# Mixers, attention, a feed-forward head and the last norm of a three-layer forward pass in another order

## The reference

```python
# first block: conformer conv, forgetting attention, short conv and pooling in parallel
mix = concatenate([y_conf, y_att, y_sc, y_pool], -1) @ w_out
h = h + rms_norm(mix, g_mix_post)
ff = square(relu(rms_norm(h, g_mlp_pre) @ w_up)) @ w_down
h = h + rms_norm(ff, g_mlp_post)
gate = sigmoid(rms_norm(h, g_ple_pre) @ w_ple_gate)
h = h + rms_norm((p @ w_ple_proj) * gate, g_ple_post)
# second block: layer 0 mixes by attention (8 latent heads, 4 differential
# heads of two maps each), layer 1 by a state-space and a gated recurrence
for l in range(2):
    m = attention_mixer(rms_norm_2(x, ...)) if l == 0 else recurrent_mixer(rms_norm_2(x, ...))
    x = x + m
    x = x + (silu(hn @ w_gate) * (hn @ w_up)) @ w_down      # width 2816
return rms_norm_2(x, norm_final)
```

## Time and profile before

| | us |
|---|---|
| runs | 1001.95, 1003.36, 999.59 |
| median | 1001.95 |
| the profiled execution's own time | 1000.06 |
| its span | 998.2 |
| PE busy | 953.5 (96%) |
| DVE busy | 700.3 (70%) |
| ACT busy | 515.8 (52%) |
| POOL busy | 87.1 (9%) |

### The profile page before, as it was taken

One profiled execution on the slowest core, in us unless ns is written; L12 is line 12 of the kernel. 1 busy time (PEld: TensorE's weight loads), 2 busy tenths in 40 slices (PEclk: granted clock), 3 DMA queues, 4 the chain that ended last, 5 costly groups with the idle time before them and its releaser, 6 DMA issues.

```text
span 998.2 us, 13575 instructions
## 1 busy us (share of the span) xinstructions
PE 953.5 (96%) x5540; PEld 835.9 (84%) x5540; DVE 700.3 (70%) x921; ACT 515.8 (52%) x698; POOL 87.1 (9%) x110
## 2 busy tenths in 40 slices
PE   6997999999999899889999999999989889999997
PEld 5996797888888688778988888888988789888886
DVE  4798785666667887886666666667979676666663
ACT  4776754444436646765543434368645355434341
POOL 4353000000000100000000000000132000000000
PEclk9999999999999999989999999999999999999999
DMA  9732365665565354224665656546321356656531
GB/s 320 245 128 92 120 220 194 199 207 183 174 206 175 112 171 143 85 85 125 215 208 173 207 171 209 169 149 211 127 85 49 121 169 211 207 172 208 172 127 43
DMA packets 106190, 164.40 MB, mean 165 GB/s; under 512 B 2816, under 2 KB 82784, under 8 KB 106000
## 3 DMA queue, kind: packets, MB, share of 16 engines
q1 hardware_dynamic: 104688, 158.25, 48.9%
q0 software_dynamic: 1440, 5.28, 1.5%
HBM read 162.47 MB, written 1.05 MB: 164 GB/s over the span
## 4 chain that ended last, share of the span: by engine, by line
PE 69%; DVE 19%; ACT 6%; issue 4%; DMA 2%; POOL 1%; DVEq 0%; POOLq 0%; ACTq 0%
PE ps L379 67%; DVE wl L1739 6%; DVE SC L1841 2%; PE ps L387 2%; ACT wh L1172 2%; DMA raw<-in_w_in 1%; DVE xhl L1744 1%; DVE xf L1748 1%; ACT junk L1160 1%; DVE st L2139 1%; ACT xhl L1178 1%; POOL st L2496 1%; DVE rows L2339 1%; DVE hs L1759 0%; DVE h L1801 0%
## 5 line engine op out<-in xcount | busy, mean ns | idle before, releaser
L1739 DVE TENSOR_TENSOR wl<-raw,wh 128x2048 fp32r<-128x2048 f32 (+2 forms) x150 | 339.6, 2266 | 153.8 <-ACT wh L1172 153.6
L1172 ACT ACTIVATE wh<-raw 128x2048 fp32r<-128x2048 f32 (+2 forms) x150 | 281.9, 1884 | 156.6 <-PE ps L379 142.8
L379 PE MATMUL ps<-xhl,wh 128*128 128x512 f32 (+1 forms) x1248 | 257.9, 354 | 2.5 <-ACT wh L1237 2.5
L379 PEld LDWEIGHTS ps<-xhl,wh 128*128 128x128 f32 x1248 | 202.4, 193 | 29.9 <-issue 3.7
L379 PE MATMUL ps<-wh,xhl 128*128 128x512 f32 (+3 forms) x1000 | 195.2, 339 | 6.0 <-ACT SC L1435 1.8
L379 PEld LDWEIGHTS ps<-wh,xhl 128*128 128x128 f32 x1000 | 155.1, 190 | 25.3 <-ACT xhl L1178 2.6
L379 PEld LDWEIGHTS ps<-xhl,wl 128*128 128x128 f32 x1008 | 135.6, 191 | 7.5
L379 PE MATMUL ps<-xhl,wl 128*128 128x256 f32 x1008 | 140.6, 282 | 0.0
L379 PE MATMUL ps<-wl,xhl 128*128 128x512 f32 (+3 forms) x500 | 105.2, 336 | 0.0
L379 PE MATMUL ps<-wh,fh 128*128 128x512 f32 x304 | 91.0, 392 | 1.8 <-DVE fl L1986 1.5
L379 PE MATMUL ps<-wh,fl 128*128 128x512 f32 x304 | 90.2, 390 | 0.0
(11 more groups left out here) (266 smaller groups left out, 840.8 us busy)
## 6 DMA issues: line engine op xcount, KB each, us to landing
raw<-in_ffn_gate SPq DMA_DIRECT2D x22, 1024.0 KB, 5.3
raw<-in_ffn_up SPq DMA_DIRECT2D x22, 1024.0 KB, 5.4
raw<-in_ffn_down SPq DMA_DIRECT2D x22, 1024.0 KB, 4.9
raw<-in_w_up SPq DMA_DIRECT2D x16, 1024.0 KB, 5.6
raw<-in_w_down SPq DMA_DIRECT2D x16, 1024.0 KB, 4.9
raw<-in_s_w_in SPq DMA_DIRECT2D x14, 1024.0 KB, 5.4
raw<-in_w_in SPq DMA_DIRECT2D x9, 1024.0 KB, 7.1
raw<-in_a_w_in SPq DMA_DIRECT2D x6, 1024.0 KB, 5.1
```

The costliest lines, as they stand in the source:

```text
L379: return e.matmul(o, a, b, start=start, stop=stop, skip_group_check=True)
L1172: e.activation(high_of(i), raw_of(i), ACT.Copy).then_inc(*up("act_high", i))
L1739: e.tensor_tensor(low_of(i), raw_of(i), high_of(i).bitcast(F32), ALU.subtract).then_inc(*up("dve_lo", i))
```

## The change

The same work is done by the same kinds of instructions, with four exceptions: four PSUM copies go from ACT to DVE, two activation table loads are added by the order on ACT, one `wl` of 128x2048 is made as two of 128x1024, and the last norm's products are shared otherwise. The rest is order, and the waits that go with it. In the diff, cut to its changed lines, the function is given ahead of each piece.

On PE: `project_end` (a wait inside it), `down_block` in halves and the order in `ffn`, `logits` and `map_back` in `attention`, `score` and `level` in `recurrent`, and the end of `recurrent`.

```diff
@@ -482 +482 @@
-def project_end(n, sl, tb, half, order):
+def project_end(n, sl, tb, half, order, x_low=None):
@@ -489,0 +490,2 @@
+            if x is xl and i == order[2] and x_low:
+                e.wait_ge(*x_low)
@@ -673 +675 @@
-    def down_block(j, tb):
+    def down_block(j, tb, halves=(0, 1)):
@@ -675 +677 @@
-        tok(down[j], [(ps[ACC[s_next][tb][c]][:, :], HALF[c]) for c in range(2)], tb, 0, j == 0, False, x)
+        tok(down[j], [(ps[ACC[s_next][tb][c]][:, :], HALF[c]) for c in halves], tb, 0, j == 0, False, x)
@@ -728,2 +730,2 @@
-        down_block(0, 0)
-        e.wait_ge(*at("dve_head", l, 1, 1))
+        down_block(0, 0, (0,))
+        e.wait_ge(*at("dve_head", l, 1, 0))
@@ -730,0 +733,2 @@
+        down_block(0, 0, (1,))
+        e.wait_ge(*at("dve_head", l, 1, 1))
@@ -732,2 +735,0 @@
-        e.wait_ge(*at("dve_head_low", l, 1, 4))
-        down_block(0, 1)
@@ -735,0 +738,2 @@
+        e.wait_ge(*at("dve_head_low", l, 1, 0))
+        down_block(0, 1)
@@ -830,0 +835,2 @@
+            e.wait_ge(*at("act_qk_turned", 1, 1, 0))
+        if i == 9:
@@ -897 +903 @@
-            e.wait_ge(*at("act_qk_turned", 1, 0, 0))
+            e.wait_ge(*at("act_qk_turned", 0, 0, 1))
@@ -1013 +1019 @@
-                e.wait_ge(*at("act_cb", tb))
+                e.wait_ge(*at("dve_cb", tb))
@@ -1028 +1034 @@
-            e.wait_ge(*at("act_xs", 0))
+            e.wait_ge(*at("dve_xs", 0))
@@ -1090 +1095,0 @@
-    feat(S["hq"][1], ps[0])
@@ -1100,0 +1106 @@
+    feat(S["hq"][1], ps[0])
@@ -1131 +1137 @@
-    e.wait_ge(*at("dve_mix3_low", 1, 0))
+    e.wait_ge(*at("act_part_high", 6, 1, 0))
@@ -1133 +1139 @@
-        project_end(6, sl, 0, half, order)
+        project_end(6, sl, 0, half, order, at("dve_mix3_low", 1, 0))
```

```diff
@@ -1312 +1318 @@
-    highs(10)
+    taps(22, 24)
@@ -1315 +1321,2 @@
-    taps(22, 26)
+    highs(10)
+    taps(24, 27)
@@ -1320 +1327 @@
-    taps(26, 29)
+    taps(27, TAPS)
@@ -1327 +1333,0 @@
-    taps(29, TAPS)
@@ -1341 +1346,0 @@
-    forget_probs(3)
@@ -1343,0 +1349 @@
+    forget_probs(3)
@@ -1561 +1567,2 @@
-    tick(7, do)
+        if c == 0:
+            tick(7, do)
@@ -1647 +1654 @@
-    for i in range(2):
+    def queries(i):
@@ -1664,0 +1672 @@
+    queries(0)
@@ -1666,3 +1673,0 @@
-    for tb in range(2):
-        e.wait_ge(*at("pe_xs", tb))
-        e.activation(xs[:, tb, :], ps[(7, 1)[tb]][:, :], ACT.Copy).then_inc(*up("act_xs", tb))
@@ -1670,3 +1674,0 @@
-    for g in range(2):
-        e.wait_ge(*at("pe_cb", g))
-        e.activation(cbs[:, g, :], ps[(2, 5)[g]][:, 0:384], ACT.Copy).then_inc(*up("act_cb", g))
@@ -1674,0 +1677 @@
+    queries(1)
@@ -1708,4 +1711,2 @@
-    for tb in range(2):
-        e.wait_ge(*at("dve_mix3_x", 1, tb))
-        part_high(4, 8, tb, (6, 1, tb))
-    norm_squares(6, 0)
+    e.wait_ge(*at("dve_mix3_x", 1, 0))
+    part_high(4, 8, 0, (6, 1, 0))
@@ -1712,0 +1714,4 @@
+    e.wait_ge(*at("dve_mix3_x", 1, 1))
+    part_high(4, 8, 1, (6, 1, 1))
+    norm_squares(6, 0)
+    highs(UP["f1"][0][1])
@@ -1726,2 +1731,6 @@
-norm_squares(7, 0)
-norm_squares(7, 1)
+for tb in range(2):
+    norm_squares(7, tb)
+    e.wait_ge(*at("pool_rstd", "norm", 7, tb))
+    e.wait_ge(*at("dve_final", tb, 1))
+    e.activation(hs[:, tb, HALF[1]], hs[:, tb, HALF[1]], ACT.Identity, scale=st[:, 3 * tb + 2:3 * tb + 3]).then_inc(
+        *up("act_out", tb))
```

```diff
@@ -1741,0 +1751,12 @@
+def low_half(i, half):
+
+    n = slots[i][1] * slots[i][2] // 2
+    c = slice(n * half, n * half + n)
+    assert i == low[0]
+    if half == 0:
+        e.wait_ge(*at("act_high", i))
+    d = e.tensor_tensor(low_of(i)[:, c], raw_of(i)[:, c], high_of(i)[:, c].bitcast(F32), ALU.subtract)
+    if half == 1:
+        d.then_inc(*up("dve_lo", i))
+        low[0] += 1
+
@@ -1910,3 +1931 @@
-    taps(11, 17)
-    lows(8)
-    taps(17, 20)
+    taps(11, 16)
@@ -1916,2 +1935 @@
-    lows(9)
-    taps(20, 23)
+    lows(8)
@@ -1919,0 +1938,2 @@
+    taps(16, 19)
+    lows(9)
@@ -1924 +1944 @@
-    taps(23, 25)
+    taps(19, 21)
@@ -1926,2 +1946 @@
-    lows(10)
-    taps(25, TAPS)
+    taps(21, TAPS)
@@ -1938 +1956,0 @@
-    mix_low(3)
@@ -1943,0 +1962 @@
+    mix_low(3)
@@ -1944,0 +1964 @@
+    lows(10)
@@ -1946 +1965,0 @@
-    lows(11)
@@ -1947,0 +1967 @@
+    lows(11)
@@ -2012 +2032 @@
-        lows(ups[3][0] + 3)
+        lows(ups[3][0] + 2)
@@ -2013,0 +2034 @@
+        lows(ups[3][0] + 3)
@@ -2016 +2036,0 @@
-        lows(down[0] + 3)
@@ -2018,0 +2039 @@
+        lows(down[0] + 3)
@@ -2165,0 +2187,4 @@
+            if i == 3:
+                low_half(S["aout"][3], 0)
+            if i == 5:
+                low_half(S["aout"][3], 1)
@@ -2226,2 +2250,0 @@
-        if t == 8:
-            lows(S["aout"][3])
@@ -2325,0 +2349,7 @@
+    lows(S["xbc"][2] + 4)
+    for tb in range(2):
+        e.wait_ge(*at("pe_xs", tb))
+        e.tensor_copy(xs[:, tb, :], ps[(7, 1)[tb]][:, :]).then_inc(*up("dve_xs", tb))
+    for g in range(2):
+        e.wait_ge(*at("pe_cb", g))
+        e.tensor_copy(cbs[:, g, :], ps[(2, 5)[g]][:, 0:384]).then_inc(*up("dve_cb", g))
@@ -2414,0 +2445,2 @@
+
+    def gated_columns_low(tb):
@@ -2417,0 +2450,3 @@
+    e.wait_ge(*at("dve_cb", 1))
+    e.wait_ge(*at("dve_dt_turned"))
+    decayed(0)
@@ -2421,0 +2457 @@
+    decayed(1)
@@ -2424,3 +2459,0 @@
-    e.wait_ge(*at("act_cb", 1))
-    decayed(0)
-    decayed(1)
@@ -2447 +2479,0 @@
-    lows(S["sout"][2])
@@ -2451 +2482,0 @@
-    state_columns(1)
@@ -2452,0 +2484,2 @@
+    state_columns(1)
+    gated_out(0)
@@ -2454,2 +2487,4 @@
-    for tb in range(2):
-        gated_out(tb)
+    gated_out(1)
+    gated_columns(0)
+    lows(S["sout"][2])
+    gated_columns_low(0)
@@ -2457,2 +2492,3 @@
-    for tb in range(2):
-        gated_columns(tb)
+    lows(UP["f1"][0][0])
+    gated_columns(1)
+    gated_columns_low(1)
@@ -2461 +2496,0 @@
-    lows(UP["f1"][0][0])
@@ -2463 +2497,0 @@
-    lows(UP["f1"][0][1])
@@ -2465 +2499 @@
-    lows(UP["f1"][1][0])
+    lows(UP["f1"][0][1])
@@ -2467 +2501 @@
-    lows(UP["f1"][1][1])
+    lows(UP["f1"][1][0])
@@ -2468,0 +2503 @@
+    lows(UP["f1"][1][1])
@@ -2484,0 +2520,3 @@
+    for c in (1, 0):
+        e.tensor_tensor(hs[:, tb, HALF[c]], h[:, tb, HALF[c]], rows[:, 1, HALF[c]], ALU.mult).then_inc(
+            *up("dve_final", tb, c))
@@ -2486,3 +2524,2 @@
-    for c in range(2):
-        e.scalar_tensor_tensor(hs[:, tb, HALF[c]], h[:, tb, HALF[c]], r, rows[:, 1, HALF[c]], ALU.mult,
-                               ALU.mult).then_inc(*up("dve_out", tb, c))
+    e.wait_ge(*at("dve_final", tb, 0))
+    e.tensor_scalar(hs[:, tb, HALF[0]], hs[:, tb, HALF[0]], r, None, ALU.mult).then_inc(*up("dve_out", tb))
@@ -2567 +2604 @@
-        e.wait_ge(*at("dve_weighed", n - 2))
+        e.wait_ge(*at("dve_weighed", max(1, n - 2)))
@@ -2601 +2638 @@
-        e.wait_ge(*at("dve_out", tb, c))
+        e.wait_ge(*(at("act_out", tb) if c else at("dve_out", tb)))
```

16 lines of the change are left out of this document (8 added, 8 removed).

## The result

The changed kernel takes 985.23 us (median of four runs, 984.29 to 985.81) against 1000.97 us of the kernel before (four runs): a ratio of 0.9839, with a 95% interval of 0.9817 to 0.9862. The forecast was 987.4, with a range of 982.0 to 996.0.

The account below looks back on a forecast made before the run. PE was taken to bound the kernel, busy 953.5 of 998.2 us, so only its idle waits could be won. Six terms summed to 14.55 us, turning the median 1001.95 into 987.4, range 982 to 996.

Parts of the forecast that it names:

- Mixer: First mixer: the conformer's mean starts at 84.8 instead of 88.47, winning 3.7 us; bounds 1.5 and 5.0.
- Head of "ff": Feed-forward head: PE's 1.53 us wait goes, a new one of 0.9 comes; net 0.65 us, from -0.7 to 1.5.
- Attention: Attention: split copies and low-part halves in DVE's gaps shorten PE's waits of 1.93 and 2.91; 3.4 us, bounds 1.5 and 4.5.
- Recurrent front: Front of recurrent layer: heads(0) 2.9 us earlier, but heads(2) limits the gain to 1.4 us; bounds -1.0 and 2.6.
- The step that named part(2) as the cause: Recurrent layer's front: DVE reaches decayed(2) at 743.6 instead of 744.8, since part(2), now waiting for weighed(1), is late.
- Recurrent tail: Tail of recurrent layer: moving wl behind needed columns removes 6.0 us of waits, adds two of 0.4; 5.2 us, bounds 3.0 and 6.0.
- Last norm: Last norm: gain products hidden under ACT's squares and POOL's power; 0.2 us won, from -0.5 to 0.5.
- which eats most of it: Last norm: POOL's power, 1.0 to 1.4 us elsewhere beside two-input DVE operations, takes most of the gain, leaving 0.2 us.
- (1): Mixer and recurrent front: DVE and POOL cost each other more than taken; gain 10.4, time 991.5; chance 0.16.
- (2): Weight stream late into "f1": the later raw load lands too late, losing the tail's 5.2; 992.7; chance 0.08.
- (3): Whole kernel: waits only move, second waits take what is freed, 3 us are left; 999; chance 0.08.
- (4): Attention or recurrent front: new gaps hold PE at 1.2 GHz; 29 us of it eats the gain, 40 gives 1007.5; chance 0.04.

Follow-up runs that it names:

- the filling products: Changed kernel plus six products of constants, overwritten by the mean, in PE's wait ahead of the conformer's mean: 983.87 us, ratio 0.9827 to the kernel before.

## Why the prediction was right, point by point

**The time.** The sum of the six terms was 14.55 us, the spans differ by 14.7, and the profiled executions' own times by 14.8 (1000.06 to 985.26). The median came out 2.2 below the forecast not through the terms but through the last step, which put the median 1.9 us above the profiled execution, as it was in three runs of the kernel before. The changed kernel's median is its profiled execution's time, within 0.03.

**Mixer, 3.7 forecast, 4.07.** Right: the turn without a wait, the mean held by the last of DVE's taps, the two small waits gone, and the hold behind the mean, put at 1.25 us and 1.09 by the filling products. PE waits there for high parts that stand behind a weight's high part on ACT; the prediction called it the third head's chain. Mis-sized: the taps. POOL ended at 81.0, not 82, and the last of DVE's ten taps ran beside an idle POOL, 0.66 us each on average (6.58/10), so the mean came at 83.9 and not 84.8. Left out: half clock behind the mean, 1.3 us in this profile. I had put the clock's fall in a rival that was to decide at 29 us of it, and not in the term itself, where a wait of 2.9 us was named by my own working. The two errors have opposite signs, so that the sum fits this well is in part luck; and the profile drew one of the two long stretches at half clock, against the median first stage the mixer gives 4.9.

**Head of "ff", 0.65, 0.79.** The new wait was put at 0.9 and is 0.70. This term was not undone by itself; the run with the mixer of before has the same 171.92.

**Attention, 3.4, 3.7.** The mix was to start at 422.7 after a wait of 2.4; shifted by the 4.84 won ahead of it, it did at 422.46 after 2.04. Both low halves were hidden. Not seen: the wait of 1.45 ahead of the turn of map 9, and that half clock shrank from 10.2 us to 3.4. PE's idle time falls by 1.5 us only; the other 2.2 are busy time, as in the upper bound, which had named the clock. The run with the attention of before has both long stretches at half clock again (414.3 to 417.8, 421.1 to 428.0). The prediction's map 7 and map 9 are the steps `tick(7)` and `tick(9)`, in which ACT takes the exponential of map 6 and DVE the maxima of map 8; no term hangs on the number.

**Recurrent front, 1.4, 1.5.** heads(0) came 3.0 us earlier, as worked out, and heads(2) 1.6, where 1.2 had been worked out. The step that named part(2) as the cause was half right: it shortens weigh(1), but undoing it costs nothing in the end. The table loads cost what their rows said.

**Recurrent tail, 5.2, 5.0.** Each of the four long waits went or shrank, the x_low wait came at 0.37, and the load that is issued later lands in time. Two small terms were wrong and offset each other in part: the two short waits of 0.9 together are not in the trace, where the stage's idle time is 5.2 in all (PE busy 55.3 of 60.5), of which the four long waits are 5.1; and the 0.4 for the wl of sout3 did not come. Without both the sum would have been 4.7.

**Last norm, +0.2, -0.3.** The only sign that was wrong. The step that failed is "which eats most of it": I had POOL's power at 1.0 to 1.4 beside DVE from other rows and still counted a gain, and did not ask what two halves that are ready at one time do to their transfers. The power took 0.93 instead of 0.55, and the last transfer landed 0.63 us behind the one before it.

**The rivals.** (1) DVE and POOL do cost each other what the rows said, but in the mixer POOL was done before it mattered. (2) No late weight: no wait for one appears in "f1". (3) The waits did not only move: PE's idle time fell from 44.8 to 33.3 us. The new or remaining ones (2.04, 1.45, 0.78, 0.72, 0.70, 0.37, 0.34, 0.22) sum to 6.6, and each of the four parts that were undone gave back its own gain. (4) PE worked as long at half clock as before, but not in the same places: the stretch at 77 us went, one behind the mean came, and that in attention shrank. At one place it was worth 0.35 to 2.4 us.

## What to carry to other kernels

Where one engine is busy 96% of the time and the rest is a dozen waits, read each wait's releaser, ask what stands ahead of that releaser in its own queue without need, and move that one piece of bulk work behind it: here most of the 14.7 us came from moving the high and low parts of weights, of 1.9 and 2.3 us, out of such places, and the parts added. Name for each wait that goes what is late next, and price the clock behind every wait that stays. Before you put a loss down to one cause, take that cause away alone and see what waits then: behind the mean a late input stood under the half clock. Undo each part alone before keeping it: one of the six was a loss. And take more than one profile before you size a part: the same stage took 113.5 to 115.1 us in nine.

## What the runs showed of the hardware that was not expected

- A wait of about 2 us may or may not cost TensorE its clock: after 1.99 us it stayed at 2.4 GHz in one profile and was at 1.2 GHz for 6.8 us in another of the same instructions, and the stage took 106.14 and 108.56 us. Likewise ahead of the old order's mean: after 3.06 us it stayed up, after 2.79 in another execution it fell.
- Behind the new order's mean it fell in all nine executions: for 3.4 us in seven of them, after waits of 2.35 to 3.49 us, and for 6.8 in two, after 3.55 and 3.60. The next projection came 0.35 us late by it in the seven, and 1.3 and 1.6 in the two.
- Three waits of 1.15 to 1.50 in place of one of 3.55 us did not keep the clock up; it fell later, on other work (3.57 us for eight products that take 2.06).
- A power of one column on GpSimd takes 0.55 us alone and 0.93 beside two products on VectorE.
- Two output transfers of 256 KB landed 0.63 us apart whether they were issued 0.66 or 0.38 us apart.
